# The low parts of the first eight weight slots move off GpSimd and VectorE

## The reference

```python
h = jnp.concatenate([jnp.broadcast_to(meta[None], (bn, N_META, D_MODEL)), x], axis=1)
...
proj = h @ w_in_ab[e]                       # 1024 -> 2048 columns
u = proj[..., :S5_WIDTH]                    # S5 state-space groups
qkv = proj[..., S5_WIDTH:].reshape(bn, seq_len, 3, SB_HEADS, SB_HEAD_DIM)
a_out = s5_mixer(u, ...)
b_out = stick_breaking_attention(qkv[:, :, 0], qkv[:, :, 1], qkv[:, :, 2])
mix = jnp.concatenate([a_out, b_out], axis=-1) @ w_out_ab[e]
```

## Time and profile before

| | us |
|---|---|
| median of 3 runs | 1346.62 (1344.17 to 1349.06) |
| the profiled execution, its own time | 1343.57 |
| its span, first to last instruction | 1341.5 |
| TensorE busy in the span | 1290.1 (96%) |
| VectorE busy | 816.1 (61%) |
| ScalarE busy | 632.0 (47%) |
| GpSimd busy | 327.2 (24%) |

### The profile page before, as it was taken

How to read it: one execution, slowest core, us unless ns; L and a number is a source line. 1 busy time by engine, 2 the same in 40 slices (tenths; PEclk the granted TensorE clock), 3 DMA queues, 4 the chain that set the end, 5 groups by cost and what they waited for, 6 DMA issues and landing times.

```text
span 1341.5 us, 23146 instructions
## 1 busy us (share of the span) xinstructions
PE 1290.1 (96%) x9766; PEld 1178.2 (88%) x9766; DVE 816.1 (61%) x1356; ACT 632.0 (47%) x982; POOL 327.2 (24%) x180
## 2 busy tenths in 40 slices
PE   6999998999999999999999999999999999999996
PEld 5998855999999999999998988877797898998984
DVE  6999654455758266384556456465557673755745
ACT  4334387435436346253465245255364463552634
POOL 1001153355210201102544123114652102011040
PEclk9999999999999999999999999999999999999997
DMA  6320100132232332323321122212222233232311
GB/s 186 95 64 33 65 1 0 64 96 64 95 96 95 95 95 95 95 95 95 95 64 64 64 64 64 63 64 95 92 66 95 95 95 99 94 123 94 100 58 63
DMA packets 109031, 108.35 MB, mean 81 GB/s; under 512 B 8096, under 2 KB 106608, under 8 KB 108928
## 3 DMA queue, kind: packets, MB, share of 16 engines
q1 hardware_dynamic: 108528, 106.77, 24.8%
q10 hardware_dynamic: 400, 0.11, 0.0%
HBM read 104.77 MB, written 2.10 MB: 80 GB/s over the span
## 4 chain that ended last, share of the span: by engine, by line
PE 81%; DVE 8%; ACT 7%; issue 2%; DMA 1%; POOL 0%; SPq 0%; DVEq 0%; ACTq 0%
PE pb L808 44%; PE pb L1011 6%; PE pb L1013 6%; PE pb L1012 6%; PE pb L974 2%; PE pb L976 2%; PE pb L975 2%; PE pb L820 1%; PE pb L914 1%; PE pb L915 1%; PE pb L852 1%; PE pb L913 1%; PE pb L1248 1%; ACT wh L1464 1%; DMA x_tok<-in_x 1%
## 5 line engine op out<-in xcount | busy, mean ns | idle before, releaser
L669 POOL TENSOR_TENSOR wl<-raw,wh 128x2048 fp32r<-128x2048 f32 x41 | 189.9, 4633 | 699.5 <-ACT wh L1464 699.5
L808 PE MATMUL pb<-hidh,wh 128*128 128x264 f32 (+1 forms) x744 | 197.8, 320 | 0.2 <-DVE wl L2111 0.2
L808 PE MATMUL pb<-hidl,wh 128*128 128x264 f32 (+1 forms) x744 | 197.4, 320 | 0.0
L808 PE MATMUL pb<-hidh,wl 128*128 128x264 f32 (+1 forms) x744 | 197.2, 319 | 0.0
L1464 ACT ACTIVATE wh<-raw 128x2048 fp32r<-128x2048 f32 x73 | 139.3, 1908 | 88.8 <-DMA raw<-in_mlp_w_down 61.4
L808 PE MATMUL pb<-hh,wh 128*128 128x264 f32 (+1 forms) x584 | 149.8, 318 | 3.4 <-DVE qd L2753 1.6
L808 PE MATMUL pb<-hh,wl 128*128 128x264 f32 (+1 forms) x584 | 145.2, 310 | 0.0
L808 PE MATMUL pb<-hl,wh 128*128 128x264 f32 (+1 forms) x584 | 145.0, 310 | 0.0
L808 PEld LDWEIGHTS pb<-hidh,wh 128*128 128x128 f32 x744 | 123.7, 188 | 10.4 <-DVE wl L2111 0.6
L808 PEld LDWEIGHTS pb<-hidh,wl 128*128 128x128 f32 x744 | 123.4, 188 | 9.7
L808 PEld LDWEIGHTS pb<-hidl,wh 128*128 128x128 f32 x744 | 123.4, 188 | 9.6
(11 more groups left out here) (471 smaller groups left out, 3256.5 us busy)
## 6 DMA issues: line engine op xcount, KB each, us to landing
raw<-in_mlp_w_up SPq DMA_DIRECT2D x32, 1024.0 KB, 5.3
raw<-in_mlp_w_down SPq DMA_DIRECT2D x32, 1024.0 KB, 5.1
raw<-in_w_in_c SPq DMA_DIRECT2D x16, 1024.0 KB, 5.3
raw<-in_w_in_ab SPq DMA_DIRECT2D x8, 1024.0 KB, 5.7
raw<-in_w_out_ab SPq DMA_DIRECT2D x4, 1024.0 KB, 5.0
raw<-in_w_out_c SPq DMA_DIRECT2D x4, 1024.0 KB, 5.1
x_tok<-in_x SPq DMA_DIRECT2D x2, 1024.0 KB, 7.9
raw<-in_s_w_glu SPq DMA_DIRECT2D x1, 1024.0 KB, 5.4
```

The source lines that it names most:

```text
L669: pool.tensor_tensor(wl[:, c % RING, :], raw[:, c % RING, :], wh[:, c % RING, :].bitcast(F32), ALU.subtract).then_inc(w_lo, 1)
L808: mm = pe.matmul(pb[:, bank + b, 0:z_ - a], lhs, rhs[:, a:z_], start=first and hi and k == 0, stop=last and k == len(todo) - 1)
```

## The change

- Slot 0's low part goes from GpSimd to VectorE, in four quarters of 512 columns (first_low), placed among the copies and hl subtractions of the last chunks. Each quarter covers two chunks of the weights.
- Tile 0 starts chunk by chunk: it waits for w_first before every second chunk instead of for the whole slot. The transposes of x now go to the banks 4 to 7. The two parameter transposes stand behind tile 0, inside turn_c, and VectorE's lin_b copy behind the last quarter.
- Slots 1 to 7: ScalarE's high(c) is followed by a second activation that writes wl = -raw, rounded to fp32r as wh is, thus -wh. GpSimd's queue then issues a DMA that adds the weights from memory to it (accum_op add), 1 MB for each slot in 1024 rows of 256 numbers, so that wl = w - wh. VectorE's seven subtractions go.

```diff
+LOWS_DMA = [*range(1, GLU)]
-LOWS_DVE = [*range(1, GLU), GLU + 1, GLU, ...
+LOWS_DVE = [GLU + 1, GLU, ...
@@ gpsimd
+            def low_dma(c):
+                pool.wait_ge(w_neg, LOWS_DMA.index(c) + 1)
+                pool.dma_start(wl[:, c % RING, :].rearrange("p (k n) -> p k n", k=KC),
+                               w_in_ab[0].rearrange("(k p) n -> p k n", p=P)[:, :, 256 * c:256 * (c + 1)], accum_op=ALU.add).then_inc(w_lo_dma[c % RING], 16)
-            low(0)
+            for c in LOWS_DMA:
+                low_dma(c)
@@ tensor
-                if c in LOWS_DVE:
+                if c in LOWS_DMA:
+                    pe.wait_ge(w_lo_dma[c % RING], 16 * (LOWS_DMA.index(c) // RING + 1))
+                elif c in LOWS_DVE:
...
+                    if not (quarters and j == 0):
+                        arrived(s0 + j)
...
+                            if quarters and t == 0 and n % 2 == 0:
+                                pe.wait_ge(w_first, n // 2 + 1)
...
-                b = 2 * (kc % 2)
+                b = 4 + 2 * (kc % 2)
...
-            pe.wait_ge(rows_in, 16 * NROWS)
-            pe.wait_ge(rows_set, 2)
-            pe.transpose(pb[:, 4, 0:P], lin_a[:, :], ident[:, :])
-            pe.transpose(pb[:, 5, 0:112], lin_b[:, :], ident[0:112, 0:112]).then_inc(rows_t, 1)
-            pe.wait_ge(xt_res, 16)
             def turn_c(t, n):
+                if t == 0 and n == KC - 1:
+                    pe.wait_ge(rows_in, 16 * NROWS)
+                    pe.wait_ge(rows_set, 2)
+                    pe.wait_ge(xt_res, 16)
+                    pe.transpose(pb[:, 4, 0:P], lin_a[:, :], ident[:, :])
+                    pe.transpose(pb[:, 5, 0:112], lin_b[:, :], ident[0:112, 0:112]).then_inc(rows_t, 1)
@@ scalar, in high(c)
+                if c in LOWS_DMA:
+                    act.wait_ge(w_hi, c + 1)
+                    act.activation(wl[:, c % RING, :], raw[:, c % RING, :], ACT.Copy, scale=-1.0).then_inc(w_neg, 1)
@@ vector
+            def first_low(k):
+                dve.wait_ge(w_hi, 1)
+                q = slice(k * SLOT // 4, (k + 1) * SLOT // 4)
+                TT(wl[:, 0, q], raw[:, 0, q], wh[:, 0, q].bitcast(F32), ALU.subtract).then_inc(w_first, 1)
...
                 if kc == KC - 1:
-                    dve.wait_ge(rows_in, 16 * NROWS)
-                    dve.wait_ge(rows_set, 1)
-                    dve.tensor_copy(lin_b[96:112, :].rearrange("a (s c) -> a s c", s=2),
...
+                    first_low(1)
...
+                if kc == 5:
+                    first_low(0)
+            first_low(2)
+            first_low(3)
+            dve.wait_ge(rows_in, 16 * NROWS)
+            dve.wait_ge(rows_set, 1)
+            dve.tensor_copy(lin_b[96:112, :].rearrange("a (s c) -> a s c", s=2),
...
-            low(1)
...
-            low(2)
...
-            low(GLU - 1)
```

More of the change, by code:

```diff
@@ L103 @@
 G = STAGES["g"][0]
-LOWS_DVE = [*range(1, GLU), GLU + 1, GLU, *[STAGES[f"down0{q}"][0] + j for q in range(4) for j in range(2)],
+LOWS_DMA = [*range(1, GLU)]
+LOWS_DVE = [GLU + 1, GLU, *[STAGES[f"down0{q}"][0] + j for q in range(4) for j in range(2)],
             *range(G + 2, G + 6), *[STAGES[f"down1{q}"][0] + j for q in range(4) for j in range(2)]]
-LOWS_POOL = [c for c in range(NSLOTS) if c not in LOWS_DVE and c not in QUAD_SLOTS]
+LOWS_POOL = [c for c in range(NSLOTS) if c and c not in LOWS_DVE and c not in LOWS_DMA and c not in QUAD_SLOTS]
 def products_before(k, m):
@@ L395, in trunk @@
         w_lo_dve = sem("w_lo_dve")
+        w_first = sem("w_first")
+        w_neg = sem("w_neg")
+        w_lo_dma = [sem(f"w_lo_dma_{r}") for r in range(RING)]
         c_copied = sem("c_copied")
@@ L821, in products_half, with run @@
                 return mm
-            def run(name, rh, rl, ready_=None, order=None, cols_=256, kcs=KC, first=0, between=None, norm=None, free=None):
+            def run(name, rh, rl, ready_=None, order=None, cols_=256, kcs=KC, first=0, between=None, norm=None, free=None, quarters=False):
                 s0, slots, t0, tiles = STAGES[name]
@@ L827, in run @@
                 for j in range(first, slots):
-                    arrived(s0 + j)
+                    if not (quarters and j == 0):
+                        arrived(s0 + j)
                     for k in range(per):
@@ L1093, in turn_c @@
                     mm.then_inc(c_turned, 1)
-            run("uqk", hh, hl, lambda n: (ready, n + 1), between=turn_c)
+            run("uqk", hh, hl, lambda n: (ready, n + 1), between=turn_c, quarters=True)
             rows_of = [slice(32 * p, 32 * p + 32) for p in range(4)]
@@ L2090, in _ @@
                 if kc == KC - 1:
-                    dve.wait_ge(rows_in, 16 * NROWS)
-                    dve.wait_ge(rows_set, 1)
-                    dve.tensor_copy(lin_b[96:112, :].rearrange("a (s c) -> a s c", s=2),
-                                    ldt[96:112, :].unsqueeze(2).broadcast_to([16, 2, 64])).then_inc(rows_set, 1)
+                    first_low(1)
                 if kc >= 1:
@@ L2099, in _ @@
                     TT(hl[:, kc - 1, :], h[:, kc - 1, :], hh[:, kc - 1, :].bitcast(F32), ALU.subtract).then_inc(ready, 1)
+                if kc == 5:
[5 more added lines that the diff above has]
+            dve.tensor_copy(lin_b[96:112, :].rearrange("a (s c) -> a s c", s=2),
+                            ldt[96:112, :].unsqueeze(2).broadcast_to([16, 2, 64])).then_inc(rows_set, 1)
             dve.wait_ge(rows_t, 1)
@@ L2233, in _ @@
             powers_times(wb.rearrange("p r k a c -> p r a k c"), CH, bb[:, 0], bb[:, 1], False, wb_ready)
-            low(3)
             dve.wait_ge(c_turned, 1)
@@ L2241, in _ @@
             dve.wait_ge(c_copied, 4)
-            powers_times(wc, 5, co[:, 0], co[:, 1], True, wc_ready, lambda: low(4))
+            powers_times(wc, 5, co[:, 0], co[:, 1], True, wc_ready)
             step(dve.tensor_copy(ew[:, 0:2, :], pt[:, 21:23, :]))
@@ L2258, in _ @@
                 n *= 2
[L2259 to L2262, removed]
                 if n < NCH:
```

## The result

| | before | after |
|---|---|---|
| median of 20 runs, us | 1345.51 (1343.24 to 1349.48) | 1349.70 (1345.78 to 1356.77) |
| the profiled execution, its own time | 1343.57 | 1349.63 |
| its span | 1341.5 | 1347.9 |

The ratio is 1.0032, with a 95% interval of 1.0020 to 1.0045: the changed kernel is 4.3 us slower (2.7 to 6.1). Forecast were +1.4 and a range of 1341.5 to 1364.

The account below looks back on a forecast made before the run. Before 23.16 us the bound was the chain through VectorE's lin_b copy, held up by GpSimd; afterwards TensorE's stream. Start -5.0, btt +1.0 and stalls +5.4 gave +1.4 us: 1345.0 us profiled, 1348.0 on the median's scale, range 1341.5 to 1364.

Parts of the forecast that it names:

- X: Slots 1 to 7: adding DMA's time from issue to landing, taken as 9.0 us, bounds 5.5 and 11.0.
- The start's working: Tile 0: starts at 17.88 us without GpSimd's subtraction and ends at 25.4 instead of 30.4, gaining 5.0 us.
- the slow pace: TensorE in tile 0: a pair every 0.44 us instead of 0.24, taken to last 3.2 us.
- VectorE's freed time carries the start's gain: At the S5 product: VectorE's 16.0 us buy nothing alone; without them the start's 5.0 us shrink to 1.5 or less.
- 3 x (X - 7.2): Slots 1 to 6, three pairs: each pair loses X beyond 7.2 us of slack once, 5.4 us in all.
- rival C: Slots 1 to 6: pieces are the price; +7.4 us at X = 11.0, up to 1.6 more per long stall; chance 33%.
- The prediction's picture of 1.4 to 1.8 us before tiles 2, 6 and 10: Uqk stage: TensorE idles that long before each of these tiles, little before tiles 4, 8 and "v".
- The btt term: Head of the S5 work: ScalarE's negation for slot 7 makes btt late, costing 1.0 us, bounds 0 and 1.9.
- B: Slots 1 to 6: the forecast itself, X between 7.2 and 9.9 us, total -4.0 to +4.1 us; chance 35%.
- A: Slots 1 to 6: adding DMA in time, X up to 7.2 us, no stall, -4.0 us, 1342.6; chance 27%.
- D: Tile 0: slow pace throughout or late quarters, gain 1.7 us instead of 5.0, 1351.3 with X = 9.0; chance 5%.
- this rival: GpSimd's DMAs: stand still while VectorE copies hold the shared port, so descriptions can't be written; no own size or chance.

Follow-up runs that it names:

- odd slots alone: Changed kernel with slots 1, 3, 5, 7 by adding DMA and 2, 4, 6 back on VectorE; 1351.13 us, ratio 1.0034 to the kernel before.
- the DMAs alone: Changed kernel with the start as before the change (slot 0 on GpSimd), slots 1 to 7 by negation and adding DMA; 1357.18 us, ratio 1.0077 to before.
- the plain DMA: Changed kernel with a plain copy instead of the adding DMA, so low parts of slots 1 to 7 are wrong; 1340.91 us, ratio 0.9962 to before.
- the two halves: Changed kernel with high part, negation and adding DMA of slots 1 to 7 in two halves of 1024 columns; 1342.15 us, ratio 0.9976 to before.
- long rows: Changed kernel whose adding DMAs read 128 rows of 8 KB of another weight matrix instead of 1024 of 1 KB; one run, 1347.36 us.
- the start alone: Changed kernel with the low parts of slots 1 to 7 back on VectorE at their old places; 1344.72 us, ratio 0.9985 to before.
- the two halves with slot 7's later: Changed kernel in two halves of 1024 columns, with ScalarE's slot 7 work moved behind b_turned(0); 1343.76 us, ratio 0.9976 to before.

## Why the prediction was right, and where it was off

**The mechanism held.** The adding DMA decides, and its X is 9.0 us as forecast. From the negation's end to when TensorE would have gone on there were 7.1 us at slot 1 (23.73 to 30.83) and 7.4 at slot 3 (51.17 to 58.6), where the forecast had 7.4 and 7.6, and the lateness is shared by pairs of slots, as odd slots alone and the DMAs alone both show. The start's working held as well: 5.5 us instead of 5.0, since the slow pace lasted 1.9 us and not the 3.2 taken; two short waits for quarters (before 20.03 and 21.87) gave some of it back. So did the step that VectorE's freed time carries the start's gain: 2.0 us were left without it (forecast up to 1.5) and 5.1 with it where the DMA is in time. That it buys nothing alone isn't shown, as no run has it alone.

**X is right by luck in its parts.** The sum was 5.5 us for the plain load and 3.4 for one more read. On GpSimd's queue the plain DMA takes 6.1 us and adding 2.9 more, and 0.7 of these 2.9 are GpSimd's longer issue, which had no term. One part was 0.6 too small, the other 0.5 too large.

**The stalls were mis-sized: 5.4 us forecast, 9.2 measured.** The step is 3 x (X - 7.2). Two things were left out of it.
- *The hand-overs.* X runs from GpSimd's issue to the landing, but the issue begins 0.3 us behind the negation (slot 3's ends at 51.17, the DMA's issue begins at 51.46), and TensorE starts some 0.2 us behind the landing, with a first pair of 0.35 instead of 0.24. The pairs of slots 3 and 4 and of 5 and 6 lost 2.5 and 2.8 us instead of 1.8, slot 1 without the slow pace 2.4. That is 2.3 us together, of which the 0.6 per stall just named explain 1.8.
- *The slow pace.* The prediction had it under rival C alone ("up to 1.6 more per long stall") and gave it no weight at X = 9.0. It came behind the first stall, of 1.98 us, and cost 1.5.

The prediction's picture of 1.4 to 1.8 us before tiles 2, 6 and 10 and "little" before the others is what the trace has for slot 3 (1.6) and not for slot 1 (2.0, with the slow pace). For "v" 1.2 us came where little was expected: slot 5's 1.6 us were less than the pair's lateness of 2.8, and slot 6 paid the rest.

**The btt term was +1.0, and 0.1 came.** Inputs(0) is 3.8 us late where "v" starts 3.7 late. Its mechanism is right, since 0.85 us of it stand in the two halves' profile and goes with high(7)'s place. In the changed kernel slot 6's stall covered it: tile 11 and with it ScalarE's copy of slot 7 were 2.5 us late, "v" 3.7. A cost that lies beside another stall is not to be added to it.

**Net.** -5.5 + 9.2 + 0.1 gives +3.8 where -5.0 + 5.4 + 1.0 gave +1.4. The start and the btt term were off in the cautious direction by 1.4 us together; the stall term was off by 3.8 in the other. The measured 4.3 lies just past the 4 us that the prediction called telling, and past B's +4.1; the prediction gave that side 0.37, mostly for C, and it came by B's mechanism at B's X.

**The rivals.** A (the DMA in time) falls with X = 9.0; what it would have given is shown by the plain DMA, -5.1 against the -4.0 worked out. The Trainium skill's "DMA: Bandwidth & Descriptors" (Anatomy of one DMA, SWDGE path) gave 4.4 us as an estimate for the plain one; this queue measured 6.1, so the page's figure is too low here even without the adding, though both would be in time. C (the pieces) falls in its mechanism: long rows save 0.7 us of the 2.9 that adding costs. Its slow pace is what came true of it. D falls with tile 0's end at 24.8. That VectorE's copies hold a GpSimd-issued DMA back, as the Trainium skill's "SBUF — State Buffer" (SBUF: two separate sides) warns, would show as a spread of the landings; it was 8.7 to 9.4 us. These two stretches (columns as above) hold one transfer with VectorE idle and one with VectorE at 97%:

```profile
88.00:99.00 11.00, 9.99 (x84) 9.78 (x83) 0.00 (x0) 2.90 (x5) 1.54 (x1) 1.00 0.70 123
...
51.00:61.00 10.00, 8.38 (x70) 8.17 (x69) 9.73 (x9) 3.01 (x4) 1.52 (x1) 1.00 0.77 122
```

Nothing of the kind shows, but the second stretch isn't the page's case: VectorE's operations in it are products and sums of two tensors (five TENSOR_TENSOR and one SCALAR_TENSOR_TENSOR of 1.49 to 1.50 us fill 9 of its 10 us), not copies. So this rival found no support, and the page's rule was not tested.

**What stays open.** The slow pace came behind idle times of 1.85, 1.98, 2.01, 2.02, 2.11, 2.12, 2.18 and 2.39 us, and not behind 1.62, nor behind 2.19 (the first stall of odd slots alone). Behind 2.01, 2.02, 2.18 and 2.39 it began 0.3 to 0.9 us after TensorE went on. The idle time alone doesn't decide it, and what else does wasn't tried. Nor was what brings the two slow stretches in the attention stage: the profiles of the start alone, of the two halves and of the plain DMA have one there (164 to 172 us), that of the two halves with slot 7's later has none.

## What to carry to other kernels

When a step of a ring's preparation moves to a slower path, write the chain for one slot from "buffer free" to "first use" with every hand-over in it, compare with the slot's period, and count the lateness once for each group of slots that wait for one another. Here 1.8 us for a pair were 2.4 to 2.8 in truth, and 3.9 where the idle time brought TensorE's slow pace back; cutting the chain in two so that copy, negation and transfer overlap turned the loss of 4 us into a gain of 3. And an engine that is idle on the path is not worthless: without VectorE's freed time 2.0 us of the start's gain were left, with it and a DMA in time 5.1.

## What the runs showed of the hardware

- An adding DMA of 1 MB from GpSimd's queue took 9.0 us from issue to landing, a plain one from the same queue 6.1, SyncE's plain load 5.5. In their middle the adding one moved 197 GB/s (28 to 31 us), the plain one 304 (26 to 29 us) and 371 at most (27 to 28 us). Half the bytes, added, took 6.3 us.
- GpSimd's own issue took 1.54 us for 1024 rows added, 0.88 for 1024 rows plain and 0.86 for 128 rows added: of these three the first alone is above 0.9 us, so neither 1024 rows nor adding was enough by itself. 512 rows added took 1.28.
- Behind eight of the nine idle times of 1.85 to 2.39 us, up to 130 us and behind the start, TensorE ran at 1.2 GHz for some 3 us, at once or up to 0.9 us later (33.0 to 36.3 in after; the clock column has 0.57 over 33 to 37). That cost 1.5 us behind a stall of 1.98.
- Behind the 4.96 us idle time at the start the same pace was seen with the clock column at 1.00, for 3.2 us; behind 4.95 us in the run with the adding DMAs alone it lasted 5.4 (23.09 to 28.46), also at 1.00; with the transposes directly in front of tile 0 it lasted 1.9.
